# Selecting experts on VectorE: one addition for the candidate sums of all heads, and a bf16 look-up with an addition tree

## The reference, cut to what matters

```python
v1, i1 = lax.top_k(s1, PEER_TOPK)
v2, i2 = lax.top_k(s2, PEER_TOPK)
cand = (v1[..., :, None] + v2[..., None, :]).reshape(T, PEER_HEADS, PEER_TOPK * PEER_TOPK)
cv, ci = lax.top_k(cand, PEER_TOPK)
a = jnp.take_along_axis(i1, ci // PEER_TOPK, axis=-1)
b = jnp.take_along_axis(i2, ci % PEER_TOPK, axis=-1)
e = a * PEER_KEYS + b
g = jax.nn.softmax(cv, axis=-1)
act = jax.nn.gelu(jnp.einsum('thkd,td->thk', u_tab[e], ht))
out = jnp.einsum('thk,thkd->td', (g * act).astype(ht.dtype), v_tab[e])
```

## Time and profile before

| | |
|---|---|
| runs | 2319.88, 2320.72, 2321.96 us; median 2320.72 |
| profiled execution, first to last instruction | 2320.1 us; its time is not listed apart from this |
| mean granted TensorE clock | 0.983 |
| TensorE busy (matmul) | 2200.6 us, 95% |
| GpSimd busy | 1749.2 us, 75% |
| VectorE busy | 1425.0 us, 61% |
| ScalarE busy | 1167.9 us, 50% |

### The profile page before, as it was taken

How to read it: one execution, slowest core, us unless ns; L and a number is a source line. 1 busy time by engine, 2 the same in 40 slices (tenths; PEclk the granted TensorE clock), 3 DMA queues, 4 the chain that set the end, 5 groups by cost and what they waited for, 6 DMA issues and landing times.

```text
span 2320.1 us, 51319 instructions
## 1 busy us (share of the span) xinstructions
PE 2200.6 (95%) x15526; PEld 1942.3 (84%) x15530; DVE 1425.0 (61%) x2318; ACT 1167.9 (50%) x2273; POOL 1749.2 (75%) x1316
## 2 busy tenths in 40 slices
PE   6999979998999999999989998899989999999998
PEld 5887868997999888888868777699989998888887
DVE  3544547996666788733346455489956667886333
ACT  5445654454444454456544455544544444545564
POOL 4745846997778788888866558569977777888886
PEclk9999999999999999999999999999999999999999
DMA  6423424454444445465554235244444444545554
GB/s 239 145 100 105 161 99 136 163 186 138 157 161 162 154 165 170 166 206 190 190 206 147 92 110 171 101 141 167 170 145 157 162 161 156 165 169 183 193 188 151
DMA packets 100517, 367.12 MB, mean 158 GB/s; under 512 B 11472, under 2 KB 11984, under 8 KB 100176
## 3 DMA queue, kind: packets, MB, share of 16 engines
q1 hardware_dynamic: 97040, 353.41, 45.6%
q10 hardware_dynamic: 3392, 12.66, 1.5%
HBM read 364.98 MB, written 1.05 MB: 158 GB/s over the span
## 4 chain that ended last, share of the span: by engine, by line
PE 45%; issue 2%; DVE 2%; POOL 1%; ACT 1%; POOLq 0%; DVEq 0%; ACTq 0%
PE acc L1066 5%; PE acc L1067 5%; PE acc L1068 5%; PE acc L1095 5%; PE acc L1097 5%; PE acc L1096 5%; PE acc L805 3%; PE acc L807 3%; PE acc L806 3%; PE aux L1034 2%; PE aux L767 1%; POOL w_lo L452 1%; PE aux L917 0%; DVE h_lo L1157 0%; PE aux L852 0%
## 5 line engine op out<-in xcount | busy, mean ns | idle before, releaser
L452 POOL TENSOR_TENSOR w_lo<-raw,w_hi 128x512 fp32r<-128x512 f32 x1312 | 1749.0, 1345 | 558.6 <-ACT w_hi L498 440.9
L498 ACT ACTIVATE w_hi<-raw 128x512 fp32r<-128x512 f32 x1344 | 841.7, 629 | 820.6 <-PE acc L1068 427.8
L1066 PE MATMUL acc<-h_hi,w_hi 128*128 128x256 f32 x2048 | 588.7, 287 | 30.8 <-POOL w_lo L452 30.8
L1067 PE MATMUL acc<-h_lo,w_hi 128*128 128x256 f32 x2048 | 580.9, 284 | 0.0
L1068 PE MATMUL acc<-h_hi,w_lo 128*128 128x256 f32 x2048 | 580.5, 283 | 0.0
L1066 PEld LDWEIGHTS acc<-h_hi,w_hi 128*128 128x128 f32 x2048 | 394.4, 193 | 33.7 <-POOL w_lo L452 33.3
L1095 PE MATMUL acc<-w_hi,eg 128*128 128x512 f32 x1024 | 406.2, 397 | 1.2 <-DVE eg L1623 1.2
L1097 PE MATMUL acc<-w_hi,eg 128*128 128x512 f32 x1024 | 399.6, 390 | 0.0
L1096 PE MATMUL acc<-w_lo,eg 128*128 128x512 f32 x1024 | 398.7, 389 | 0.0
L1067 PEld LDWEIGHTS acc<-h_lo,w_hi 128*128 128x128 f32 x2048 | 394.9, 193 | 0.1
L1068 PEld LDWEIGHTS acc<-h_hi,w_lo 128*128 128x128 f32 x2048 | 394.4, 193 | 0.0
(11 more groups left out here) (229 smaller groups left out, 2234.0 us busy)
## 6 DMA issues: line engine op xcount, KB each, us to landing
raw<-stream_dram SPq DMA_DIRECT2D x672, 512.0 KB, 3.3
big<-parb_dram ACTq DMA_DIRECT2D x2, 2128.0 KB, 9.6
big<-mem_dram ACTq DMA_DIRECT2D x3, 1024.0 KB, 5.3
big<-pm_dram ACTq DMA_DIRECT2D x2, 768.0 KB, 13.4
big<-parr_dram ACTq DMA_DIRECT2D x2, 640.0 KB, 10.7
X<-x_dram ACTq DMA_DIRECT2D x1, 1024.0 KB, 11.9
out_dram<-X SPq DMA_DIRECT2D x1, 1024.0 KB, 4.0
big<-lnrow_dram ACTq DMA_DIRECT2D x2, 256.0 KB, 11.3
```

Of the source, the lines that this page charges most:

```text
L452: nc.gpsimd.tensor_tensor(w_lo[:, k % SLOTS, :], raw[:, k // PER_CHUNK, k % PER_CHUNK, :], w_hi[:, k % SLOTS, :].bitcast(F32), ALU.subtrac ...
L498: nc.scalar.activation(w_hi[:, k % SLOTS, :], raw[:, (k // PER_CHUNK) % RAW, k % PER_CHUNK, :], ACT.Copy).then_inc(hi_ready, 1)
L1066: pe_.matmul(acc[:, q, 0:S], wh, h_hi[:, kt, :], start=(kt == 0), stop=False)
L1067: pe_.matmul(acc[:, q, 0:S], wh, h_lo[:, kt, :], start=False, stop=False)
```

## The change

- The eight additions of candidate sums (one for each head, 256 elements) become one of 2048 elements for each token tile.
- `tf` and `iab` become bf16, laid out by factor, rank, head, so that the heads are innermost. The cast of `topi` and the two casts to `iab` read with strides for that.
- Both factors are looked up together: one comparison of 4096 bf16 elements, one multiplication of 4096, and in place of the reduction a tree of additions of 2048, 1024, 512 and 256 elements; the last writes f32 to `ab`. All values are whole numbers below 256. So six instructions stand where six stood.
- A constant tile `ranks` (0 to 15, repeated for both factors and 8 heads) is made once at the start of the kernel, behind `iota_b`, and the wait for `zero_set` counts it.

```diff
+        ranks = sb("ranks", [P, 2, TOPK, PH], BF16)
...
-        onehot = rout[:, :].rearrange("p (m j) -> p m j", j=TOPK)
+        onehot = rout[:, :].bitcast(BF16).rearrange("p (f j m) -> p f j m", f=2, j=TOPK)
...
-        tf = topf[:, :].rearrange("p (h f k) -> p h f k", h=PH, f=2)
-        iab = topv[:, :].rearrange("p (w m) -> p w m", w=2)
+        tf = topf[:, 0:128].bitcast(BF16).rearrange("p (f k h) -> p f k h", f=2, k=TOPK)
+        iab = topv[:, 0:128].bitcast(BF16).rearrange("p (f k h) -> p f k h", f=2, k=TOPK)
...
-            dve.wait_ge(zero_set, 2)
+            V.tensor_copy(ranks[:, :, :, :], iota16.unsqueeze(1).unsqueeze(3).broadcast_to((P, 2, TOPK, PH))).then_inc(zero_set, 1)
+            dve.wait_ge(zero_set, 3)
...
-                    d.step(V.tensor_copy(topf[:], topi[:]))
-
-                    for h in range(PH):
-                        d.step(V.tensor_tensor(cand[:, h], tv[:, h, 0, :].unsqueeze(2).broadcast_to((P, 16, 16)),
-                                               tv[:, h, 1, :].unsqueeze(1).broadcast_to((P, 16, 16)), ALU.add))
+                    d.step(V.tensor_copy(tf, ti.rearrange("p h f k -> p f k h")))
+
+                    d.step(V.tensor_tensor(cand, tv[:, :, 0, :].unsqueeze(3).broadcast_to((P, PH, 16, 16)),
+                                           tv[:, :, 1, :].unsqueeze(2).broadcast_to((P, PH, 16, 16)), ALU.add))
...
+                    cik = cia.rearrange("p (h k) -> p k h", h=PH)
                     d.step(V.tensor_scalar(cia, ci, 4, None, ALU.logical_shift_right))
-                    d.step(V.tensor_copy(iab[:, 0, :], cia))
+                    d.step(V.tensor_copy(iab[:, 0], cik))
                     d.step(V.tensor_scalar(cia, ci, 15, None, ALU.bitwise_and))
-                    d.step(V.tensor_copy(iab[:, 1, :], cia))
-                    for f in range(2):
-                        d.step(V.tensor_tensor(onehot, iab[:, f, :].unsqueeze(2).broadcast_to((P, 128, 16)),
-                                               iota16.unsqueeze(1).broadcast_to((P, 128, 16)), ALU.is_equal))
-                        oh = onehot.rearrange("p (h k) j -> p h k j", h=PH)
-                        d.step(V.tensor_tensor(oh, oh, tf[:, :, f, :].unsqueeze(2).broadcast_to((P, PH, 16, 16)), ALU.mult))
-                        d.step(V.tensor_reduce(ab[:, f, t].rearrange("p h k -> p (h k)"), onehot, AX.X, ALU.add))
+                    d.step(V.tensor_copy(iab[:, 1], cik))
+
+                    d.step(V.tensor_tensor(onehot.rearrange("p f j (k h) -> p f j k h", h=PH),
+                                           iab.unsqueeze(2).broadcast_to((P, 2, 16, 16, PH)),
+                                           ranks[:, :, :, :].unsqueeze(3).broadcast_to((P, 2, 16, 16, PH)), ALU.is_equal))
+                    oh = onehot.rearrange("p f j (k h) -> p f j k h", h=PH)
+                    d.step(V.tensor_tensor(oh, oh, tf.unsqueeze(3).broadcast_to((P, 2, 16, 16, PH)), ALU.mult))
+                    for n in (8, 4, 2):
+                        d.step(V.tensor_tensor(onehot[:, :, 0:n], onehot[:, :, 0:n], onehot[:, :, n:2 * n], ALU.add))
+                    d.step(V.tensor_tensor(ab[:, :, t].rearrange("p w h k -> p w k h"), oh[:, :, 0], oh[:, :, 1], ALU.add))
```

## The result

The changed kernel takes 2300.03 us (2298.22 to 2301.31, four runs) against 2321.34 before: 21.3 us less, ratio 0.990, interval 0.9888 to 0.9911. The forecast was 2298, with a gain of 22.5 us. On a second chip it was 2299.74 against 2323.19, ratio 0.9899 (0.9884 to 0.9914). The profiled execution took 2299.59 us, its span is 2297.8.

What follows compares the result with a forecast made beforehand. TensorE, busy 95% of the span, was taken as the bound; its losses fall from 18.4 to 7.0 us per layer, 22.8 for two, less 0.3 at the start: 2298 us from 2320.72, range 2287 to 2313.

Steps and rivals of the forecast that it cites:

- The stall for `cv_ready`: Expert selection: TensorE's 8.27 us wait, priced 8.4 plus 1.95 for lowered clock, vanishes as `cv_ready` comes before ScalarE asks.
- The look-up: Expert selection: bf16 priced by bytes; TensorE stalls 2.8 us per tile, against 4.9 and 3.1 before the change.
- The candidate sums: Merged addition of 2048 elements per tile: holds GpSimd 2.13 us, costing TensorE 0.2 us per tile.
- the lead: Weight-piece chain: GpSimd runs 2.07 us ahead of TensorE's need, absorbing that much delay; regained at 0.19 us a piece.
- The detour of ScalarE: ScalarE's table loads, exponential and small operations before its next `w_hi`: 3.07 us late, costing 1.0 us per layer.
- The sum: Lost TensorE time per layer falls from 18.4 to 7.0 us; two layers gain 22.8, less 0.3 at the start.
- 0.3 us at the start: Kernel start: the added cast of 256 elements behind `iota_b` costs 0.15 to 0.3 us, taken as 0.3.
- After key 64 nothing changes: Rest of the sweep: VectorE makes slots behind TensorE's transposes, still eight keys ahead of use, so no time change.

Runs made afterwards that it cites:

- single-edit kernels: Kernel before with only the merged candidate addition: 2309.44 us, ratio 0.9942; changed kernel with the eight candidate additions per tile back: 2310.84 us, ratio 0.9945.
- f32 variant: Changed kernel with `iab` and `tf` in f32, one-hots and addition tree still bf16: 2320.44 us, ratio 0.9986 to the kernel before.
- six kernels with the tile: Changed kernel, its versions with eight additions back, f32 operands, look-up by factor, additions issued twice, and the kernel before plus only `ranks`: 2297.98 to 2325.07 us.
- PSUM variant: Changed kernel with `tf` and ranks as f32 in PSUM, both tiles' scores copied up front, no `ranks` tile in SBUF: 2288.16 us, ratio 0.9844.

## Why the prediction was right

**The stall for `cv_ready`**: right in mechanism and size. I had `cv_ready` at 516 and ScalarE asking at 531; it was 520.2 and 531.0. Of the 4 us 3.0 are waits for GpSimd inside the new operations: the merged addition took 3.30 and the look-up 13.7, where I had 2.9 and 12.6. The sweep also began 0.7 us later, and the last subtraction took 0.84 and not 0.42. The margin of 11 us hid that. The price of the old stall was 10.9 with everything that follows it, against 8.4 + 1.95. Both single-edit kernels show that it was lateness: each makes VectorE earlier and shortens the wait.

**The look-up**: right. The bytes decided the price of bf16, not the count of elements, and the f32 variant shows that this was the choice that mattered: slow forms of only the two longest operations left 3 of the 23 us. I had 2.8 us lost per tile, it was 2.9; GpSimd's operations 3.4, 3.3, 2.3, 1.7, they were 3.16, 3.32, 2.26, 1.75. For the old look-ups I had 4.9 and 3.1, they were 5.33 and 3.48: I counted the waits and left out that the first matmul behind one starts its successor 0.22 us later and not 0.12, and the small shift ahead of the first wait.

**The candidate sums**: priced at 0.2 per tile, they cost nothing; the GpSimd operation beside was 3.16 and not 3.42 us, since VectorE's turn had begun while the one before ran. Issued twice they cost 1.74, so the hold is there and the lead swallows it.

**The detour of ScalarE**: I had 1.0 us; the wait is 0.84 and the loss 1.1. The 1.64 of the table take in the transposes, which cost about 0.6 before the change as well.

**The sum.** Per layer 18.4 to 7.0 forecast, 19.9 to 7.6 measured: 11.4 against 12.3. The weak step is what I took for the stretches outside the sweeps: 0.3 us at the start and nothing else, where 2 to 3 us were lost on the first chip (1.0 on the second). "After key 64 nothing changes" holds for the sweep itself, whose second half takes 209.49 us in all 14 profiles. The 0.3 us at the start can't be confirmed: TensorE's first matmul is at 13.21 and 13.41 in the two profiles of before, at 13.52 and 13.42 in the two of the changed kernel. Too small a gain in the sweeps and too small a loss outside them have opposite signs, and by that luck 2298 was so near 2300.

**Open**: why the extra tile makes TensorE wait 0.4 us longer for `h_lo` in each layer, and what decides whether the clock is lowered in a given stretch between the sweeps. That the six kernels with the tile lose 0.9 to 1.9 us is seen; 0.8 of it is accounted for.

## What to carry to other kernels

An engine off the path can cost twice: by when it is done, and by what it holds while it works; look for both, since the same edit moves them differently. Beside a busy GpSimd, price a VectorE operation by its number of SBUF operands first and by its length second: a look-up with two operations of 4.42 us that read one operand from PSUM cost nothing here, where one with two of 2.3 us and both operands in SBUF cost 2.9. And before an edit makes one long hold of many short ones, work out the lead of the chain that it holds: here 2.07 us, which covers one hold of 2.13 but not two.

## What the runs showed of the hardware

- VectorE and GpSimd take turns, one operation each, while both want the SBUF port: GpSimd's period became 3.3, 2.2, 1.7 and 1.5 us behind holds of 2.13, 1.07, 0.53 and 0.27 (1.44 is its period without them).
- bf16 `tensor_tensor` with all operands in SBUF kept its double pace with operands broadcast over a middle dimension and runs of only 8 elements: 3.27 us with a wait of 1.0 for 4096 elements. One f32 operand of the three took it away (5.37).
- TensorE's granted clock fell from the upper level of 2.4 GHz to 1.2 (matmuls of 256 columns 0.21 us apart, not 0.12) in or behind waits of 8.27, 4.73 and 3.71 us, and stayed up behind most of 1.74 and less. The length of one wait didn't decide it: in the second layer of the f32 variant the clock was down straight behind a wait of 1.74, and behind the same waits the PSUM variant had 1.00 in one profile and 0.72 in the other.
